# A weight stream of 591 slabs: TensorE waits for and releases each slab by halves, two token tiles in turn

## The chip, the cores and the metric

The kernel runs on one NeuronCore of a Trainium2 chip. The metric is the device time of one execution, in microseconds (us). Its engines are named as the profile names them: PE is TensorE (matmuls), with PEld for its weight loads; ACT is ScalarE; DVE is VectorE; POOL is GpSimd; SP is SyncE, which issues the loads of the weight stream.

## The reference

Two models of depth 2 run one after the other on one sequence of 256 tokens of width 1024, in float32. The first model's layer is a mixer (nine projections of 1024 columns, a gated recurrence over 8 heads, a short convolution, gates, an output projection) and a feed-forward part: dense in layer 0, and a mixture of 8 experts with the top 2 in layer 1. The second model's layer is feed-forward, mixer (gated MLP, pooling, sparse attention with a top-k, a convolution of 31 taps, four branches merged), feed-forward.

```python
def swiglu(h, w1, w3, w2):
    a = jnp.einsum('bsd,df->bsf', h, w1)
    b = jnp.einsum('bsd,df->bsf', h, w3)
    return jnp.einsum('bsf,fd->bsd', jax.nn.silu(a) * b, w2)

def moe_swiglu(h, router_w, w1, w3, w2):
    ...
    for e in range(N_EXPERTS):
        a = t @ w1[e]
        b = t @ w3[e]
        out = out + gates[:, e:e + 1] * ((jax.nn.silu(a) * b) @ w2[e])
    return out.reshape(bsz, seq, d)
```

What matters here is that all weights, some 620 MB, are read once, and that each is used in a matmul with few tokens.

## The kernel before

**The weight stream.** All large weights are laid out ahead of the launch as one array `W` of 591 slabs in the order of use. A slab is 128 partitions x 2048 float32 (`SLAB`), 1.05 MB, in two halves of 1024 columns (`HALF`), each loaded by a DMA of its own. A slab of an up or input projection holds four blocks of 512 columns (`CW`), one for each of four blocks of 128 of the contraction; the projection to 512 output columns takes two such slabs (`half` 0 and 1). A slab of a down projection holds two blocks of 128 rows with all 1024 output columns each, so that each half is one block of rows.

**Three engines handle each slab.** A float32 product is made of three matmuls in fp32r: the weight is split into a rounded high part and the rest, and the activations too, and high x high, high x low and low x high are added up in PSUM. For this SP loads a half into `raw` (`Sync.slabs`, L256 to L266), ACT copies it to `whi` in fp32r (`Scalar.hi`, L289 to L302), DVE subtracts `raw - whi` into `wlo` (`Vector.lo`, L727 to L738), and PE runs the three matmuls for each block and tile (`Tensor.slab`, L1299 to L1310). `raw`, `whi` and `wlo` have three slots each (`RING`), and ACT and DVE run two slabs ahead of PE (`LEAD`). The order in each engine's queue is written out by hand, so that an engine that waits for a slab holds up everything behind it.

**Who waits for whom.** There are four counters. A landing counts up `land{slot}{half}`. ACT's copy of a half waits for its landing and counts up `act_hi`. DVE's subtraction of a half waits for `act_hi` and counts up `dve_lo`. SP's load of a half waits for `dve_lo` of the same half three slabs earlier. So these three already work by halves. PE doesn't: it waits once for both halves of a slab (`dve_lo` at 2n + 2, L1304) and counts up `pe_slab` once, at the slab's last matmul (L1309); ACT waits for `pe_slab` of the slab three earlier before it copies either half (L297).

**How PE uses a slab.** `terms` is a list of (PSUM bank, high activations, low activations, columns of the slab, first, last). `columns` (L1312) makes it for up and input projections, `rows` (L1319) for down projections; two further lists stand in the mixer of the second model (its index projection and its branches). In all of them the token tile (128 tokens) is the outer loop and the block of the slab the inner one. Dense stages have two tiles, so 8 terms and 24 matmuls for a slab of an input projection; the experts gather their tokens into one tile, so 4 terms and 12 matmuls. Each tile accumulates in a bank of its own. An event that tells an evacuation that its banks are ready is always given with a slab's last matmul.

**The stages.** In order: the first mixer (48 slabs, `mixer1`), the dense feed-forward part (33), the mixer again (48), the experts (8 x 33 = 264 slabs), then for both layers of the second model feed-forward (33), mixer (33, `mixer2`), feed-forward (33). A feed-forward part is 22 slabs up and 11 down. In `up`, ACT does for every pair of slabs: two `hi`, the copy of the turned gate product of the pair before (L480), the SiLU of this pair (`gate`, L470 to L473), which waits for the pair's last matmul; DVE does two `lo`, the low part of the turned product (L943) and the product of the gate (L933 or L935). In the experts, PE also adds the previous expert's output into its tokens' places: `scatter` (L1551, L1552) with two matmul pairs for each tile, after the first pair of slabs for tile 0 and after the whole up projection for tile 1, and DVE adds the result to `X` (L993), in DVE's order behind the last `lo` and gate of the up projection. The down projection of the experts uses those banks, so PE waits for L993 before it starts. In the second model's mixer, DVE works through a top-k (L1162 to L1166) and through 31 taps of a convolution (L1179, L1182), with one `lo` after every six taps; PE needs the finished convolution at L1660.

The half of the stream that is ACT's, as it stands:

```python
            slot = self.slot()
            if self.n >= RING:
                act.wait_ge(k.of("pe_slab"), self.n - RING + 1)
            for h in range(2):
                part = slice(h * HALF, (h + 1) * HALF)
                act.wait_ge(k.of(f"land{slot}{h}"), 16 * (self.n // RING + 1))
                act.activation(k.whi[:, slot, part], k.raw[:, slot, part], ACT.Copy).then_inc(*k.up("act_hi"))
```

Of the kernel before, what the change touches and what calls it, by code (L numbers as in the profile page):

```python
# [38 lines left out]
HALF = SLAB // 2  # L39
RING = 3  # L40
# [245 lines left out]
class Scalar(Engine):  # L286

    def hi(self, count=1):  # L289

        act, k = self.eng, self.k
        for _ in range(count):
            if self.n == self.limit:
                return
            slot = self.slot()
            if self.n >= RING:
                act.wait_ge(k.of("pe_slab"), self.n - RING + 1)  # L297
            for h in range(2):
                part = slice(h * HALF, (h + 1) * HALF)
                act.wait_ge(k.of(f"land{slot}{h}"), 16 * (self.n // RING + 1))  # L300
                act.activation(k.whi[:, slot, part], k.raw[:, slot, part], ACT.Copy).then_inc(*k.up("act_hi"))  # L301
            self.n += 1  # L302
# [993 lines left out]
class Tensor(Engine):  # L1296

    def slab(self, terms, event=None):  # L1299

        pe, k = self.eng, self.k
        slot = self.slot()
        pe.wait_ge(k.of("dve_lo"), 2 * self.n + 2)  # L1304
        for ps, xh, xl, cols, first, last in terms:
            pe.matmul(ps, xh, k.whi[:, slot, cols], start=first, stop=False)  # L1306
            pe.matmul(ps, xh, k.wlo[:, slot, cols], start=False, stop=False)  # L1307
            mm = pe.matmul(ps, xl, k.whi[:, slot, cols], start=False, stop=last)  # L1308
        mm.then_inc(*k.up("pe_slab", event))  # L1309
        self.n += 1  # L1310

    def columns(self, half, bank, XH, XL, tiles=NT, step=1):  # L1312
# [735 lines left out]
```

## Time and profile before

| | |
|---|---|
| three runs | 3104.79, 3109.59, 3114.94 us; median 3109.59 |
| the profiled execution | 3106.7 us |
| its span, from the first to the last instruction | 3104.9 us |
| mean granted TensorE clock | 0.965 |
| busy: PE, PEld | 2898.1 us, 2376.6 us (13334 instructions each) |
| busy: DVE, ACT, POOL | 2062.2, 1696.0, 32.9 us |
| moved by DMA | 633.63 MB, mean 204 GB/s |
| the slabs' loads | 1182 of 512 KB, median 5.2 us from issue to landing |

All rows are of the one profiled execution. Its time is 1.8 us above its span, and 2.9 us below the median of the three runs. Matmuls are pipelined: a matmul's own length in the rows (0.39 us) is longer than the distance from its start to the next one's, and it is this distance, the pitch, that says how fast TensorE goes. The granted clock is a share of full speed: 1.00 is 2.4 GHz, 0.50 is 1.2 GHz.

### The profile page before, as it was taken

How to read it: one execution, taken by the hardware profiler on the slowest of the kernel's cores; microseconds unless marked ns; L12 is line 12 of the kernel's file. 1: busy time of each engine (PE TensorE's matmuls, PEld its weight loads, DVE VectorE, ACT ScalarE, POOL GpSimd, SP SyncE). 2: the span in 40 equal slices, each digit the busy share in tenths (PEclk: the TensorE clock that was granted, in tenths of full speed). 3: DMA queues.
4: the chain of work that ended last, by engine and by line, in shares of the span. 5: the costliest groups of instructions: out<-in, count | busy, mean ns of one | idle time of the engine just before them, and what ended most of it. 6: DMA issues, size and time to landing. Idle time of an engine off the chain costs nothing.

```text
span 3104.9 us, 34324 instructions
## 1 busy us (share of the span) xinstructions
PE 2898.1 (93%) x13334; PEld 2376.6 (77%) x13334; DVE 2062.2 (66%) x2910; ACT 1696.0 (55%) x2271; POOL 32.9 (1%) x55
## 2 busy tenths in 40 slices
PE   8998899999887999999999989989899999898998
PEld 6887688788765878777877768877778788776786
DVE  5566655656664898889888955468655455587553
ACT  5645354555523777677767754455454444555543
POOL 0000000000001000000000000000000000000000
PEclk9998899999987999999999989999999999999999
DMA  6443455454333999999989965544455555444453
GB/s 220 149 135 114 132 178 188 155 166 140 122 128 112 350 349 333 323 333 345 330 318 344 343 234 183 187 143 153 146 170 185 170 189 187 144 162 149 157 186 112
DMA packets 173658, 633.63 MB, mean 204 GB/s; under 512 B 19521, under 2 KB 19521, under 8 KB 173489
## 3 DMA queue, kind: packets, MB, share of 16 engines
q1 hardware_dynamic: 170752, 621.88, 59.0%
q0 software_dynamic: 2736, 9.49, 0.9%
q8 instruction: 107, 1.75, 0.2%
q14 instruction: 63, 0.51, 0.0%
HBM read 629.20 MB, written 2.10 MB: 203 GB/s over the span
## 4 chain that ended last, share of the span: by engine, by line
PE 78%; DVE 12%; DMA 4%; ACT 4%; issue 1%; SPq 0%; DVEq 0%; ACTq 0%; POOLq 0%
PE ps L1306 24%; PE ps L1308 23%; PE ps L1307 23%; DVE wlo L737 4%; DMA raw<-in_W 4%; PE ps L1418 2%; DVE CA L1182 2%; ACT whi L301 1%; PE ps L1495 1%; PE ps L1542 1%; PE ps L1338 1%; PE ps L1405 0%; PE ps L1404 0%; DVE XN L905 0%; DVE Z L1269 0%
## 5 line engine op out<-in xcount | busy, mean ns | idle before, releaser
L737 DVE TENSOR_TENSOR wlo<-raw,whi 128x1024 fp32r<-128x1024 f32 x1182 | 1394.0, 1221 | 560.4 <-ACT whi L301 550.8
L301 ACT ACTIVATE whi<-raw 128x1024 fp32r<-128x1024 f32 x1182 | 1197.8, 1057 | 600.8 <-PE ps L1308 547.7
L1306 PE MATMUL ps<-whi,XH 128*128 128x512 f32 (+1 forms) x2192 | 873.4, 398 | 41.2 <-DVE XL L755 17.3
L1307 PE MATMUL ps<-wlo,XH 128*128 128x512 f32 (+1 forms) x2192 | 859.0, 392 | 0.0
L1308 PE MATMUL ps<-whi,XL 128*128 128x512 f32 (+1 forms) x2192 | 859.0, 392 | 0.0
L1306 PEld LDWEIGHTS ps<-whi,XH 128*128 128x128 f32 x2192 | 418.8, 191 | 134.9 <-DVE XL L755 21.8
L1308 PEld LDWEIGHTS ps<-whi,XL 128*128 128x128 f32 x2192 | 417.6, 191 | 87.5
L1307 PEld LDWEIGHTS ps<-wlo,XH 128*128 128x128 f32 x2192 | 418.9, 191 | 82.8 <-issue 0.5
L1306 PE MATMUL ps<-whi,XEH 128*128 128x512 f32 x704 | 284.2, 404 | 1.4 <-DVE XEL L986 1.4
L1308 PE MATMUL ps<-whi,XEL 128*128 128x512 f32 x704 | 278.4, 395 | 0.0
L1307 PE MATMUL ps<-wlo,XEH 128*128 128x512 f32 x704 | 278.0, 395 | 0.0
L1306 PE MATMUL ps<-whi,GH 128*128 128x512 f32 x440 | 174.9, 397 | 0.0
L1308 PE MATMUL ps<-whi,GL 128*128 128x512 f32 x440 | 174.0, 395 | 0.0
L1307 PE MATMUL ps<-wlo,GH 128*128 128x512 f32 x440 | 174.0, 395 | 0.0
L1306 PE MATMUL ps<-whi,GH_ 128*128 128x512 f32 x352 | 147.8, 420 | 16.5 <-DVE X L993 16.5
L1308 PEld LDWEIGHTS ps<-whi,XEL 128*128 128x128 f32 x704 | 132.2, 188 | 31.6
L1306 PEld LDWEIGHTS ps<-whi,XEH 128*128 128x128 f32 x704 | 132.4, 188 | 30.0 <-DVE XEL L986 1.6
L1307 PEld LDWEIGHTS ps<-wlo,XEH 128*128 128x128 f32 x704 | 132.5, 188 | 28.7
L480 ACT ACTIVATE GH<-ps 128x512 fp32r<-128x512 f32 x55 | 32.9, 598 | 207.5 <-PE ps L1495 207.5
L943 DVE TENSOR_TENSOR GL<-ps,GH 128x512 fp32r<-128x512 f32 x55 | 38.0, 691 | 162.9 <-ACT GH L480 162.9
L1307 PE MATMUL ps<-wlo,GH_ 128*128 128x512 f32 x352 | 141.0, 400 | 0.0
L1308 PE MATMUL ps<-whi,GL_ 128*128 128x512 f32 x352 | 140.8, 400 | 0.0
(358 smaller groups left out, 2467.9 us busy)
## 6 DMA issues: line engine op xcount, KB each, us to landing
raw<-in_W SPq DMA_DIRECT2D x1182, 512.0 KB, 5.2
GP<-in_ffn_post_g POOLq DMA_DIRECT2D x4, 512.0 KB, 4.0
X<-in_x SPq DMA_DIRECT2D x1, 1024.0 KB, 5.0
skew<-RB POOLq DMA_DIRECT2D x4, 256.0 KB, 2.8
RB<-skew POOLq DMA_DIRECT2D x8, 128.0 KB, 2.5
GP<-in_mix_post_g POOLq DMA_DIRECT2D x2, 512.0 KB, 3.8
out<-X SPq DMA_DIRECT2D x1, 1024.0 KB, 4.0
mload<-in_cum_sums POOLq DMA_DIRECT2D x1, 768.0 KB, 8.5
```

The costliest lines, as they stand in the source:

```text
L301: act.activation(k.whi[:, slot, part], k.raw[:, slot, part], ACT.Copy).then_inc(*k.up("act_hi"))
L480: act.activation(GH[:, 2 * g:2 * g + 2, :], src, ACT.Copy).then_inc(*k.up("act_split", f"{T}.gh{g}"))
L737: dve.tensor_tensor(k.wlo[:, slot, part], k.raw[:, slot, part], k.whi[:, slot, part], ALU.subtract).then_inc(*k.up("dve_lo"))
L943: dve.tensor_tensor(GL[:, 2 * g:2 * g + 2, :], src, GH[:, 2 * g:2 * g + 2, :], ALU.subtract).then_inc(*k.up("dve_split", f"{T}.gl{g}"))
L1182: x = dve.scalar_tensor_tensor(out=CA[:, c, :], in0=HP[:, c, j:j + S], scalar=dw(c, j), in1=CA[:, c, :], op0=ALU.mult, op1=ALU.add)
L1306: pe.matmul(ps, xh, k.whi[:, slot, cols], start=first, stop=False)
L1307: pe.matmul(ps, xh, k.wlo[:, slot, cols], start=False, stop=False)
L1308: mm = pe.matmul(ps, xl, k.whi[:, slot, cols], start=False, stop=last)
L1338: mm = pe.transpose(bank[:, i * S + t * P:i * S + (t + 1) * P], src(2 * b + i, t), k.ident[:])
L1418: mm = pe.matmul(o, x, x, start=True, stop=True)
L1495: mm = pe.transpose(turned[:, fb, t * P:(t + 1) * P], GN[:, t, fb * P:(fb + 1) * P], k.ident[:])
L1542: mm = pe.matmul(k.ps[:, 6 + c // 4, (c % 4) * P:(c % 4 + 1) * P], k.XN[:, t, c * P:(c + 1) * P], k.PM[:, t, :], start=t == 0, stop=t == N ...
```

## The change

ACT waits for `pe_slab` ahead of each half in place of once for the slab, and the counter goes up by two for a slab. PE walks a slab's terms in two passes, one for each half of its columns. Ahead of each pass it waits for `dve_lo` of that half alone, and the last matmul of each pass counts up `pe_slab`; a stage's event stays with the second pass. With two tiles the order of the matmuls turns from tile 0 (all blocks), tile 1 (all blocks) to tile 0, tile 1 (the first half's blocks), tile 0, tile 1 (the second half's). With one tile it stays as it was. The matmuls themselves, their number and what they read and write are the same, and so are all loads, copies and subtractions.

```diff
@@ Scalar.hi
             slot = self.slot()
-            if self.n >= RING:
-                act.wait_ge(k.of("pe_slab"), self.n - RING + 1)
             for h in range(2):
                 part = slice(h * HALF, (h + 1) * HALF)
+                if self.n >= RING:
+                    act.wait_ge(k.of("pe_slab"), 2 * (self.n - RING) + h + 1)
                 act.wait_ge(k.of(f"land{slot}{h}"), 16 * (self.n // RING + 1))
                 act.activation(k.whi[:, slot, part], k.raw[:, slot, part], ACT.Copy).then_inc(*k.up("act_hi"))
@@ Tensor.slab
-        pe.wait_ge(k.of("dve_lo"), 2 * self.n + 2)
-        for ps, xh, xl, cols, first, last in terms:
-            pe.matmul(ps, xh, k.whi[:, slot, cols], start=first, stop=False)
-            pe.matmul(ps, xh, k.wlo[:, slot, cols], start=False, stop=False)
-            mm = pe.matmul(ps, xl, k.whi[:, slot, cols], start=False, stop=last)
-        mm.then_inc(*k.up("pe_slab", event))
+        for h in range(2):
+            pe.wait_ge(k.of("dve_lo"), 2 * self.n + h + 1)
+            for ps, xh, xl, cols, first, last in terms:
+                if cols.start // HALF != h:
+                    continue
+                pe.matmul(ps, xh, k.whi[:, slot, cols], start=first, stop=False)
+                pe.matmul(ps, xh, k.wlo[:, slot, cols], start=False, stop=False)
+                mm = pe.matmul(ps, xl, k.whi[:, slot, cols], start=False, stop=last)
+            mm.then_inc(*k.up("pe_slab", event if h else None))
         self.n += 1
```

## Rows read from the trace of the kernel before

**Rows 1.** The page, parts 1 and 4: busy time, and the chain that ended last

```profile
PE 2898.1 (93%) x13334; PEld 2376.6 (77%) x13334; DVE 2062.2 (66%) x2910; ACT 1696.0 (55%) x2271; POOL 32.9 (1%) x55
...
PE 78%; DVE 12%; DMA 4%; ACT 4%; issue 1%; SPq 0%; DVEq 0%; ACTq 0%; POOLq 0%
```

**Rows 2.** The page, part 5: busy us, mean ns | idle before, releaser

```profile
L737 DVE TENSOR_TENSOR wlo<-raw,whi 128x1024 fp32r<-128x1024 f32 x1182 | 1394.0, 1221 | 560.4 <-ACT whi L301 550.8
L301 ACT ACTIVATE whi<-raw 128x1024 fp32r<-128x1024 f32 x1182 | 1197.8, 1057 | 600.8 <-PE ps L1308 547.7
```

**Rows 3.** TensorE's waits: us in total, times, longest us

```profile
PE ps L1306 <- DVE X L993: 16.5, 7, 3.1
...
PE ps L1306 <- DVE wlo L737: 7.3, 4, 2.0
```

**Rows 4.** Windows: PE, PEld, DVE, ACT, POOL busy, then PEclk, DMA share, GB/s

```profile
400.00:480.00 80.00, 80.00 (x368) 66.28 (x367) 43.79 (x49) 36.74 (x50) 0.00 (x0) 1.00 0.59 193
1119.00:1149.00 30.00, 30.00 (x136) 24.20 (x135) 27.59 (x33) 24.48 (x32) 0.00 (x0) 1.00 0.99 369
1170.00:1190.00 20.00, 20.00 (x100) 16.64 (x99) 16.14 (x15) 13.08 (x14) 0.00 (x0) 1.00 0.89 298
```

**Rows 5.** Timeline of TensorE, dense up projection: start us, us

```profile
481.22 0.39 PE L1308 MATMUL ps<-whi,XL 128*128 128x512 f32 x1
481.44 0.39 PE L1306 MATMUL ps<-whi,XH 128*128 128x512 f32 x1
...
483.94 0.39 PE L1308 MATMUL ps<-whi,XL 128*128 128x512 f32 x1
484.16 0.39 PE L1306 MATMUL ps<-whi,XH 128*128 128x512 f32 x1
...
489.96 0.48 PE L1306 MATMUL ps<-whi,XH 128*128 128x512 f32 x1
490.28 0.39 PE L1307 MATMUL ps<-wlo,XH 128*128 128x512 f32 x1
```

**Rows 6.** Timeline of ScalarE, experts: two gates of an up projection, a down projection

```profile
1141.34 0.39 ACT L480 ACTIVATE GH_<-ps 128x256 fp32r<-128x256 f32 x1 [0.60 <-PE ps L1495]
...
1147.14 0.39 ACT L480 ACTIVATE GH_<-ps 128x256 fp32r<-128x256 f32 x1 [0.55 <-PE ps L1495]
...
1174.09 2.01 ACT L301 ACTIVATE whi<-raw 128x1024 fp32r<-128x1024 f32 x2 [1.24 <-PE ps L1308]
```

**Rows 7.** Timeline of ScalarE, VectorE, TensorE where an up projection ends

```profile
1252.58 2.20 ACT L301 ACTIVATE whi<-raw 128x1024 fp32r<-128x1024 f32 x2 [0.23 <-PE ps L1308]
...
1260.01 2.01 ACT L301 ACTIVATE whi<-raw 128x1024 fp32r<-128x1024 f32 x2 [1.86 <-DMA raw<-in_W]
...
1261.10 2.36 DVE L737 TENSOR_TENSOR wlo<-raw,whi 128x1024 fp32r<-128x1024 f32 x2 [1.50 <-ACT whi L301]
...
1264.05 1.22 DVE L993 TENSOR_TENSOR X<-ps,X 128x1024 f32<-128x1024 f32 x1
...
1261.90 0.40 PE L1552 MATMUL ps<-YL,PT 128*128 128x512 f32 x1
1265.36 0.47 PE L1306 MATMUL ps<-whi,GH_ 128*128 128x512 f32 x1 [3.06 <-DVE X L993]
```

**Rows 8.** Timeline of VectorE and TensorE, convolution of the second model's mixer

```profile
2117.39 2.36 DVE L737 TENSOR_TENSOR wlo<-raw,whi 128x1024 fp32r<-128x1024 f32 x2
2119.67 5.45 DVE L1182 SCALAR_TENSOR_TENSOR CA<-HP,pc,CA 128x256 f32<-128x256 f32 x12
...
2119.90 0.47 PE L1306 MATMUL ps<-whi,XH 128*128 128x512 f32 x1 [1.69 <-DVE wlo L737]
...
2136.14 1.13 PE L1660 MATMUL ps<-CA,ones 128*128 128x256 f32 x4 [2.79 <-DVE CA L1182]
```

**Rows 9.** Timeline of TensorE after an expert's stall, at half clock

```profile
1370.52 0.63 PE L1308 MATMUL ps<-whi,GL_ 128*128 128x512 f32 x1
1370.95 0.63 PE L1306 MATMUL ps<-whi,GH_ 128*128 128x512 f32 x1
```

## The prediction, made before the changed kernel ran

> **What bounds the kernel now.** The page comes first. TensorE is busy for 2898 of 3105 us, and most of the chain that ended last is its own matmuls; VectorE has 12% of that chain, DMA and ScalarE 4% each [rows 1]. So time can be won only in TensorE's 207 idle us (3105 - 2898), in stretches at half clock, or by cheaper matmuls. The stream that the change touches is the 1182 half slabs: a load of 512 KB (128 x 1024 numbers of 4 bytes), a ScalarE copy of 1.06 us and a VectorE subtraction of 1.22 us for each. ScalarE stood idle 548 us for TensorE before its copies, VectorE 551 us for ScalarE [rows 2]. Those two figures look like the prize, but idle time of an engine counts only if TensorE then waits for it. The view of TensorE's own waits says how often it does: 4 waits and 7.3 us for a subtraction of the stream, and 7 waits and 16.5 us for the add of L993, which stands behind the stream in VectorE's order [rows 3]. The rest of its idle time is for norms, transposes and splits that no slab feeds.
>
> Next the windows by stage. In a dense stage (two token tiles) DMA is busy 0.59 of the time and TensorE all of it; in the experts (one tile, half the matmuls for the same bytes) DMA is busy 0.99 at 369 GB/s in the up projection and 0.89 in the down projection [rows 4]. A slab is 1.05 MB. In the up projection the copies L480 ahead of two gates start 5.80 us apart, at 1141.34 and 1147.14 [rows 6], which is two slabs: 2.1 MB in 5.8 us ask for 361 GB/s, nearly what DMA gives. So the experts are the only place where the stream is nearly as slow as TensorE.
>
> **The change, part by part.** (1) **Marks.** 591 slabs get one more wait and one more signal in TensorE's stream. A wait that has been met and a signal already stand at each slab's end: the matmul at 483.94 signals, the one at 484.16 has waited, and the pitch is 0.22 us, as it is inside a slab (481.22 to 481.44) [rows 5]. I take 0. The clock of the rows reads to 0.01 us, so the bound is 0.01 x 591 = 5.9 us slower, and there is no reason for a gain. The Trainium skill speaks against the change here ("TensorE: Matmul & The Clock Gate", The cost: per-tile semaphore tail): there each further signal on a matmul adds some 26 ns, which would be 591 x 0.026 = 15 us; the rows above show no such step at the signals that are there already, though those come at the end of a slab too.
>
> (2) **Order of the matmuls.** The same 24 matmuls of a dense slab run as tile 0, tile 1, tile 0, tile 1 in place of tile 0, tile 1, so there are two more changes of bank in 327 slabs. The change of tile is just the pair 481.22 to 481.44, 12 matmuls before the slab's end [rows 5], with no step in it. I take 0; bound 654 x 0.01 = 6.5 us slower. In the experts the order stays. Banks are signalled ready only by a slab's last matmul, before and after, so no evacuation comes earlier.
>
> (3) **Earlier release, dense stages.** The copy of a slab's first half may start half a slab (2.7 us) earlier, the second half's as before; ScalarE then has 1.06 us less left after the slab's end, VectorE finishes about 1.1 us earlier, and SyncE's next load, which waits for that subtraction, goes out as much earlier. DMA has room for it at 0.59 [rows 4], and GpSimd's few loads are far off. What is queued behind on ScalarE (gates, evacuations) waits for the end of a later slab anyhow. TensorE doesn't wait for slabs there, as two lie ready ahead. Worth 0; the cover is that lead of a slab or more, some 5 us against about 3.5 us of copy and subtraction. A loss is excluded, since nothing is asked to be ready sooner than before.
>
> (4) **Mixer of the second block, twice.** Here VectorE is the bound: a slab's two subtractions (2.36) and twelve taps of the convolution (5.45) make 7.8 us against 5.45 us of matmuls. TensorE waits for two slabs, 1.69 us for the first (four such waits in both mixers make up the 7.3 us) [rows 3], and then 2.79 us for the last tap [rows 8]. With half waits it starts each of the two slabs one subtraction (1.14 us) earlier. But the next work needs VectorE's last tap, whose time doesn't move, as those subtractions don't wait for ScalarE. So 4 x 1.14 = 4.6 us are won and all given back in a longer idle of about 3.9 us before L1660. I take 0. A longer idle may bring a stretch at half clock: bound 1.5 us slower for each mixer (priced below).
>
> (5) **Experts.** In the down projection ScalarE waits 1.24 us for a slab's end before a pair of copies [rows 6]; that goes, and the stream gets about 1.2 us ahead, where nobody is waiting. What counts is the end of the up projection: TensorE's last scatter starts at 1261.90, the add L993 runs only at 1264.05, behind two late subtractions, and TensorE resumes at 1265.36, after 3.06 us idle [rows 7]. Back from there: the subtractions at 1261.10 waited for a copy, and that for a load (1.86 us), not for TensorE. Over the whole up projection ScalarE's first copy of a pair follows its gate, which waits for a whole slab; only the second one waits for TensorE, and for 0.23 us [rows 7]. The lead won in the down projection is lost again at these gates, since three slots can't hold more. I take 0.2 us for each of 7 stalls: 1.4 us faster. The far bound: if VectorE were never late, the idle would be the add behind the last scatter, about 1.22 plus 0.1 us, so 16.5 - 7 x 1.3 = 7.4 us to win, and the half clock that follows three of the seven stalls. At half clock the pitch is 0.43 instead of 0.23 us [rows 9]; over the 3.3 us that such a stretch lasts that is 3.3 x (1 - 0.23/0.43) = 1.5 us, three times 4.5. Together 12 us faster; the near bound is 0.
>
> **Sum.** The profiled execution took 3106.7 us (span 3104.9 and 1.8 around it): 3106.7 - 1.4 = 3105.3. The median of the three runs is 2.9 us above it, so 3108.2, say **3108**. A difference under 0.3% (9.3 us) can't be told from no change here: the runs shown spread over 10 us.
>
> **Rivals.** *A: the experts' stalls go.* If the DMA engines are kept busy from the down projection on, the lead isn't lost and the late loads land before they are asked for. For it: 0.89 in the down projection, so there is room, and loads that are late at its end [rows 4, 7]. Against: loads wait for slots, slots for gates. It gives the 12 us of (5): 3109.6 - 12 = 3098, and it is the only way that I see to a clear gain. Chance 0.17.
>
> *B: the half clock comes to more stalls.* The change moves idle time about: shorter before slabs, longer before L1660. Of the seven expert stalls four were followed by full clock, and so were some four of like length in the two mixers. Were all eight to fall, 8 x 1.5 = 12 us slower: 3120. It decides once six of them fall and none of the others is spared. For it: stalls of like length come with and without half clock, so it turns on little. Against: chance works both ways, and the experts' stalls don't grow. Chance 0.06.
>
> *C: a mark in the middle of a slab costs.* If the array ran empty at the signal or the weight load couldn't go ahead past the wait, each would cost up to what the dearest spot between matmuls of a slab shows: after the transposes the pitch is 0.32 (489.96 to 490.28) instead of 0.23 [rows 5], 0.09 x 591 = 53 us, 3161. The pitch of 0.22 over a signal and a met wait in the same rows speaks against it. By the skill's 26 ns above it would be some 3123. Chance 0.03.
>
> *D: nothing reaches TensorE at all*, (5) included: 3109.6, within my forecast. The forecast with D has 0.74.
>
> **How the numbers follow.** Faster by over 0.3% is A: 0.17. Slower is B and C: 0.09. Same 0.74. The range takes in most of A below and part of B and the bounds of (1) and (2) above: 3097 to 3117.
>
> **What would show it.** Right: ScalarE's idle time for TensorE before L301 falls from 548 us by roughly 200 to 300, and that doesn't reach the span; TensorE's wait for wlo falls from 7.3 to about 3 us and its wait for CA L1182 grows by as much; the seven waits for L993 stay at 15 to 17 us; the pitch over the new mark is 0.22 to 0.23; DMA in the up projection stays at 0.99. Wrong: the waits for L993 fall near 9 us (A), windows of the experts with a lower granted clock (B), a step at the twelfth matmul (C), or more busy time of TensorE for the same 13334 matmuls.

## The result and the profile after

The changed kernel took 3118.19 us (median of 8 runs, 3113.66 to 3124.32), the kernel before 3111.07 us (8 runs, 3101.48 to 3119.64). The ratio is 1.0027, with the interval 1.0014 to 1.004. The means of the eight runs lie 8.4 us apart, so the change loses about 8 us. That is less than the 0.3% (9.3 us) under which the prediction said that nothing could be told from no change; with eight runs of each kernel the interval reaches some 4 us to either side, and it doesn't hold 1. The time is 1 us above the range of 3097 to 3117. The same kernel timed once more (below) gave 1.0024.

The page of the changed kernel: its head, the busy times and the chain that ended last.

```profile
span 3115.6 us, 34912 instructions
...
PE 2904.3 (93%) x13334; PEld 2381.7 (76%) x13334; DVE 2067.9 (66%) x2910; ACT 1707.3 (55%) x2271; POOL 32.9 (1%) x55
...
PE 75%; DVE 15%; DMA 5%; ACT 4%; issue 1%; SPq 0%; ACTq 0%; DVEq 0%; POOLq 0%
```

Against [rows 1] two things stand out. TensorE has the same 13334 matmuls but is busy 6.2 us longer (2904.3 against 2898.1), and in the chain 3% have gone from TensorE to VectorE. The second isn't the loss: a kernel below without the loss has TensorE at 75% too. The granted clock says where most of the 6.2 us come from: 235 us of the span are at half clock, 222 before, and there the pitch is 0.43 us in place of 0.23 [rows 9]. By stage, TensorE is busy 2.3 us longer in the experts (6.9 us more at half clock) and 4.0 us longer behind them (13.3 us more). TensorE's idle time grew by the rest, from 207 to 211 us. The two add up to the 10.7 us by which the span grew.

The same page, the two groups of the slabs' preparation (busy us, mean ns | idle before, releaser).

```profile
L737 DVE TENSOR_TENSOR wlo<-raw,whi 128x1024 fp32r<-128x1024 f32 x1182 | 1401.1, 1223 | 475.0 <-ACT whi L301 465.2
L301 ACT ACTIVATE whi<-raw 128x1024 fp32r<-128x1024 f32 x1182 | 1210.7, 1061 | 509.5 <-PE ps L1311 396.7
```

ScalarE's idle time for TensorE fell from 547.7 to 396.7 us and VectorE's for ScalarE from 550.8 to 465.2 [rows 2], and nothing of it reached the span. What reached it stands in TensorE's own waits (us in total, times, longest):

```profile
PE ps L1309 <- DVE X L993: 20.2, 7, 5.0
...
PE ps L1663 <- DVE CA L1182: 7.9, 2, 4.0
...
PE ps L1309 <- DVE wlo L737: 6.2, 4, 2.0
```

The seven waits for L993, at the end of each expert's up projection, are 20.2 us in place of 16.5 [rows 3]. The worst, 5.03 us, in the timeline of ScalarE, VectorE and TensorE after the change (start us, us; in brackets the idle time before):

```profile
1572.56 1.06 ACT L301 ACTIVATE whi<-raw 128x1024 fp32r<-128x1024 f32 x1 [0.86 <-DMA raw<-in_W]
...
1573.65 2.52 DVE L737 TENSOR_TENSOR wlo<-raw,whi 128x1024 fp32r<-128x1024 f32 x2 [0.70 <-ACT whi L301]
1573.85 1.06 ACT L301 ACTIVATE whi<-raw 128x1024 fp32r<-128x1024 f32 x1 [0.23 <-DMA raw<-in_W]
...
1576.74 1.22 DVE L993 TENSOR_TENSOR X<-ps,X 128x1024 f32<-128x1024 f32 x1
...
1578.06 0.77 PE L1309 MATMUL ps<-whi,GH_ 128*128 128x512 f32 x1 [5.03 <-DVE X L993]
```

It is the stall of [rows 7], only longer: a load lands late, ScalarE copies behind it, VectorE subtracts behind that, and the add of L993 that TensorE needs stands last. Both of the last two copies waited for their loads. The 0.77 us of the first matmul behind it, in place of 0.47 in [rows 7], is the half clock.

What is new shows in the chain that ended last, ahead of that stall (start us, us, what), here of the changed kernel:

```profile
1566.76 7.01 DMA raw<-in_W
1573.77 0.02 issue
1573.79 0.02 ACTq L300
1573.80 0.04 issue
1573.85 1.07 ACT whi L301
```

A second half's copy in the kernel before:

```profile
1145.37 6.47 DMA raw<-in_W
1151.84 0.02 issue
1151.86 1.07 ACT whi L301
```

Before, this copy starts 0.02 us after its load has landed. Now an instruction of ScalarE's queue (`ACTq L300`, the wait for the landing) stands between, and the copy starts 0.08 us after. The reason is in the instruction counts.
```profile
span 3104.9 us, 34324 instructions
```

which is one for each slab from the fourth on (591 - 3): the wait for `pe_slab` that the second half now has. And of the two waits, the one written last (the landing) is the separate instruction, L300, while the copy itself carries the wait for `pe_slab`, long met where the load is late. In the kernel before only the first halves had two waits, and its chain shows the separate one there:

```profile
1773.87 5.95 DMA raw<-in_W
1779.82 0.02 issue
1779.84 0.02 ACTq L300
1779.85 0.04 issue
1779.90 1.07 ACT whi L301
```

Over all copies that a load held, the trace of before has a mean of 0.088 us from landing to copy for first halves and 0.023 for second ones, that of after 0.082 and 0.081.

Whether these 0.06 us matter depends on how often a load holds a copy. ScalarE's waits before L301 (us in total, times, longest), kernel before:

```profile
ACT whi L301 <- PE ps L1308: 547.7, 247, 7.2
...
ACT whi L301 <- DMA raw<-in_W: 48.3, 90, 1.9
```

and changed kernel:

```profile
ACT whi L301 <- PE ps L1311: 396.7, 274, 4.2
...
ACT whi L301 <- DMA raw<-in_W: 111.8, 202, 2.7
```

The waits for loads went from 90 to 202. Copies asked for earlier meet loads that can't come earlier; that isn't all of it, as the kernel below that only adds the second wait has 166 and 143 in its two profiles. The window 1511 to 1577, the up projection of the experts with the longest stall (busy us of PE, PEld, DVE, ACT, POOL with counts, then PEclk, DMA share, GB/s), before:

```profile
1511.00:1577.00 66.00, 63.92 (x286) 51.22 (x284) 61.65 (x68) 52.44 (x67) 0.00 (x0) 1.00 0.97 352
```

and after:

```profile
1511.00:1577.00 66.00, 62.01 (x275) 49.01 (x273) 58.18 (x66) 49.70 (x64) 0.00 (x0) 0.99 0.95 338
```

DMA is less busy and moves 338 in place of 352 GB/s. Loads that are issued later would look like this: SyncE's next load into a slot waits for the subtraction, that for the copy, and that for the landing. The experts as a whole, from the start of their first matmul with XEH to the start of their last with GH_, took 823.8 us before and 829.5 after. What lies behind the experts grew by 5.4 us in these two executions, from 1286.7 to 1292.1.

### The profile page after: what moved, and what is told of

Its sections match the earlier page's. It is cut to its first block, busy times and chain, and to the rows that moved or that the text cites. A ratio compares the mean times of both kernels' runs of the same rounds, so it can differ in the third digit from the quotient of the medians.

```text
span 3115.6 us, 34912 instructions
## 1 busy us (share of the span) xinstructions
PE 2904.3 (93%) x13334; PEld 2381.7 (76%) x13334; DVE 2067.9 (66%) x2910; ACT 1707.3 (55%) x2271; POOL 32.9 (1%) x55
## 4 chain that ended last, share of the span: by engine, by line
PE 75%; DVE 15%; DMA 5%; ACT 4%; issue 1%; SPq 0%; ACTq 0%; DVEq 0%; POOLq 0%
PE ps L1309 22%; PE ps L1311 22%; PE ps L1310 22%; DVE wlo L737 6%; DMA raw<-in_W 5%; PE ps L1421 2%; DVE CA L1182 2%; ACT whi L301 1%; PE ps L1498 1%; PE ps L1545 1%; PE ps L1341 1%; PE ps L1408 0%; PE ps L1407 0%; DVE XN L905 0%; DVE Z L1269 0%
## 5 line engine op out<-in xcount | busy, mean ns | idle before, releaser
L737 DVE TENSOR_TENSOR wlo<-raw,whi 128x1024 fp32r<-128x1024 f32 x1182 | 1401.1, 1223 | 475.0 <-ACT whi L301 465.2
L301 ACT ACTIVATE whi<-raw 128x1024 fp32r<-128x1024 f32 x1182 | 1210.7, 1061 | 509.5 <-PE ps L1311 396.7
L1309 PE MATMUL ps<-whi,XH 128*128 128x512 f32 (+1 forms) x2192 | 872.7, 398 | 40.5 <-DVE XL L755 17.8
L1309 PEld LDWEIGHTS ps<-whi,XH 128*128 128x128 f32 x2192 | 418.8, 191 | 133.9 <-DVE XL L755 21.9
L1309 PE MATMUL ps<-whi,XEH 128*128 128x512 f32 x704 | 284.4, 404 | 1.4 <-DVE XEL L986 1.4
L1309 PE MATMUL ps<-whi,GH 128*128 128x512 f32 x440 | 174.9, 397 | 0.0
L1309 PE MATMUL ps<-whi,GH_ 128*128 128x512 f32 x352 | 148.6, 422 | 20.2 <-DVE X L993 20.2
L1309 PEld LDWEIGHTS ps<-whi,XEH 128*128 128x128 f32 x704 | 132.4, 188 | 30.9 <-DVE XEL L986 1.6
```

The source lines that it names most:

```text
L737: dve.tensor_tensor(k.wlo[:, slot, part], k.raw[:, slot, part], k.whi[:, slot, part], ALU.subtract).then_inc(*k.up("dve_lo"))
```

## The experiments

All kernels compute the whole of the reference. Each was timed in five rounds against the kernel before on the same chip; beside the median stands the ratio with its interval. "Experts" is that stretch in the one profiled execution of a kernel; it scatters by several us between executions (all its values stand in a table at the end of this section), so the ratios decide. The kernel before measured 3108.1 to 3111.3 us (medians) in these series.

### The parts, one at a time

*ScalarE's second wait alone.* The kernel before, with its own met wait for `pe_slab` asked again ahead of the second half:

```
-            if self.n >= RING:
-                act.wait_ge(k.of("pe_slab"), self.n - RING + 1)
             for h in range(2):
...
+                if self.n >= RING:
+                    act.wait_ge(k.of("pe_slab"), self.n - RING + 1)
                 act.wait_ge(k.of(f"land{slot}{h}"), ...)
```

> TensorE as before. Only ScalarE waits a second time, ahead of a slab's second half, for the count it has already seen. Theory 1 (the added wait of ScalarE costs): in the changed kernel's profile a copy of a second half that waits for its load starts 0.08 us after the landing, before it was 0.02; here it must be 0.08 too, the up projections of the experts move about 340 GB/s in place of 351, the seven waits for L993 come to about 20 us in place of 16.5, and the time is 4 to 7 us above before (ratio 1.0013 to 1.0023). Theory 2 (the half clock and the mixer's longer stall cost, ScalarE's wait nothing): ratio 1.000, waits for L993 16 to 17 us.

Measured: 3110.23 us, ratio 1.0004 (0.9995 to 1.0013). Landing to copy is 0.08 us for both halves, the waits for L993 are 19.3 us and the experts 832.8, as in the changed kernel, but the time doesn't follow: theory 1 had asked for 1.0013 or more. Once more:

> The kernel before with ScalarE's second, met wait, once more. Theory 1: experts 828 to 834 us, ratio 1.001 to 1.002. If the first timing (1.0004) holds and the experts come out at 825 here, the second wait costs only together with the earlier copies of the change.

3111.53 us, 1.0005 (0.9994 to 1.0016), and this time the waits for L993 are 16.8 us and the experts 826.0, with the same 0.08 us from landing to copy. The wait by itself measures 1 to 2 us, and the intervals reach from nothing to 5 us.

*TensorE's half waits and the order of tiles, one mark a slab.* As the change, with `mm.then_inc(...)` once, behind the loop over `h`, and ScalarE as before.

> TensorE waits by halves and takes two tiles in turn, but signals once a slab, and ScalarE waits once. Theory 1: the waits for L993 as before, 16 to 17 us, DMA in the up projections 351 GB/s; the wait of L1663 or its like for the last tap grows from 2.8 to 3.95 us in both mixers, and the whole is 0 to 3 us slower. Theory 2: this carries nearly all of the loss, 6 to 9 us (ratio 1.002 to 1.003), with more stretches at half clock than before (24, 221.7 us in total).

3113.58 us, 1.001 (0.9999 to 1.0021): 3 us, with an interval from 0 to 6.5 us. Theory 2, which put 6 to 9 us here, is out at all but its lower end.

*The marks without use.* TensorE waits for whole slabs (`2 * self.n + 2`), tiles in turn, a mark after each half; ScalarE waits once a slab, for `2 * (self.n - RING) + 2`.

> TensorE takes two tiles in turn and signals each half, but waits for whole slabs, and ScalarE waits once, for the second mark. So ScalarE's and VectorE's work comes when it did before. If a mark in the middle of a slab costs TensorE nothing (forecast): pitch across the mark 0.22 to 0.23 us, experts 822 to 826, ratio within 0.9995 and 1.0005. If each costs some 0.02 us (rival C at the skill's figure): TensorE's busy time 10 us or more up and the ratio above 1.003.

3110.95 us, 1.0007 (0.9995 to 1.0019). 591 more signals and the new order measure 2 us, 6 at most.

*The marks used.* The changed kernel, but TensorE waits for whole slabs.

> The changed kernel, but TensorE waits for whole slabs. ScalarE has its two waits, and copies a first half once half the slab is used. Theory 1: experts 828 to 833 us and the waits for L993 19 to 21 us, as in the changed kernel; the waits for the last tap (L1182) back at 2.8 us; ratio 1.001 to 1.0025. If the half waits of TensorE are what costs: ratio 1.000 to 1.0005.

3111.22 us, 1.0009 (0.9998 to 1.002).

*By place.* The whole change for the experts' 264 slabs alone, then for all the others alone (a helper counts the marks; it decides on `MOE_BASE <= n < MOE_BASE + NE * FF_SLABS`).

> The whole change, but for the 264 slabs of the experts alone. Theory 1: 4 to 7 us slower, waits for L993 near 20 us. Theory 2: within 1 us of before, since neither the order of the matmuls nor the convolution's stall is touched.

> The whole change, but for the 327 slabs outside the experts alone. Theory 1: 1 to 4 us slower (the mixers' part); waits for L993 16 to 17 us. Theory 2: 6 to 9 us slower. If both parts cost, this and the kernel with the experts alone add up to the 7 to 8 us of the whole.

Experts alone: 3113.51 us, 1.0013 (1.0003 to 1.0023). The rest alone: 3109.3 us, 1.0004 (0.9995 to 1.0014). So a loss shows where the stream is nearly as slow as TensorE, and none is seen in the dense stages and the second model's mixers. But the two together make 1.0017, less than the whole change's 1.0027 and 1.0024. The intervals leave room for an equal sum; whether the parts cost more together than one by one isn't settled by these runs.

*TensorE's half waits in the second model's mixers alone* (66 slabs, one mark a slab):

> The kernel before, but TensorE waits by halves, and takes two tiles in turn, in the two mixers of the second model (66 slabs), with one mark a slab. If the longer idle ahead of the last tap and the half clock behind it are the second cost: waits for CA L1182 grow from 2.8 to 3.95 us (or come earlier with a half clock stretch between), the part behind the experts takes 1288 to 1290 us in place of about 1286, ratio 1.0003 to 1.001. If they aren't: 1286 and 1.000.

3110.33 us, 1.0006 (0.9994 to 1.0018). TensorE's waits for the stream and for the last tap (L1665 is L1660 of the kernel before):

```profile
PE ps L1311 <- DVE wlo L737: 5.1, 4, 2.0
PE ps L1665 <- DVE CA L1182: 4.7, 2, 2.4
```

The wait for the last tap didn't grow to 3.95 us but came out at 2.3 and 2.4, with a stretch at half clock 9 us ahead of it, the case that the expectation had in brackets. The part behind the experts took 1285.6 us, so it lost nothing.

### The order of two waits

*The change with the landing asked first.* This is the experiment that decides. Two source lines change places, nothing else:

```
             for h in range(2):
                 part = slice(h * HALF, (h + 1) * HALF)
+                act.wait_ge(k.of(f"land{slot}{h}"), 16 * (self.n // RING + 1))
                 if self.n >= RING:
                     act.wait_ge(k.of("pe_slab"), 2 * (self.n - RING) + h + 1)
-                act.wait_ge(k.of(f"land{slot}{h}"), 16 * (self.n // RING + 1))
```

The instructions are as many (34912). Only, now the wait for `pe_slab` is the separate one and the copy itself waits for the landing.

> The changed kernel with ScalarE's two waits ahead of each copy in the other order: landing first, then TensorE's mark. In the traces so far a copy held up by its load starts 0.08 us after the landing where it has two waits and 0.02 where it has one. Theory 1 (the second wait stands between landing and copy as an instruction of its own): with the landing waited for by the copy itself the 0.08 falls to about 0.02 for both halves, the experts take 822 to 826 us as in kernels whose ScalarE wasn't touched (824, 826, 822) and not 830 to 833, and the whole is at 1.000 to 1.0015 of before. Theory 2 (marks and order in the experts cost by themselves): experts at about 830 and the ratio at 1.0027 as in the changed kernel.

3107.14 us, 0.9993 (0.998 to 1.0006): the loss is gone. Its chain (start us, us, what):

```profile
1143.75 6.71 DMA raw<-in_W
1150.46 0.02 issue
1150.48 1.07 ACT whi L301
```

ScalarE's waits in it,

```profile
ACT whi L301 <- PE ps L1311: 400.2, 275, 4.3
ACT whi L301 <- DMA raw<-in_W: 92.8, 194, 2.0
```

TensorE's wait for L993 in it,

```profile
PE ps L1309 <- DVE X L993: 15.9, 7, 3.1
```

and the window of before:

```profile
1511.00:1577.00 66.00, 63.10 (x282) 50.65 (x281) 60.99 (x68) 51.84 (x66) 0.00 (x0) 1.00 0.96 348
```

The copy follows its load by 0.02 us again. ScalarE still waits 194 times for a load, as with the change, yet TensorE's waits for L993 are 15.9 us, the rate is 348 GB/s, and the experts take 822.8 us. So it is not that copies are asked for earlier that costs, but in which order the two waits stand. What the order changes in the trace is only where the 0.06 us go: copies held by TensorE's mark now start 0.085 us after it, in place of 0.022 with the change as it was, and those held by a load start 0.023 us after it, in place of 0.08. The same delay costs nothing behind TensorE's mark.

Both kernels again, on another chip and beside each other:

> The changed kernel itself, once more, so that it and the next one are timed in the same rounds. If the loss is real: ratio 1.0015 to 1.0035, landing to copy 0.08 us, experts 828 to 832 us. If the first measurement was partly luck: below 1.001.

> The changed kernel with the landing waited for by the copy itself, once more beside it. Theory 1: 0.999 to 1.001, at least 4 us below the changed kernel in the same rounds; experts 822 to 827 us. Theory 2: the same as the changed kernel.

The change 3117.64 us, 1.0024 (1.0012 to 1.0036); landing first 3110.87 us, 1.001 (0.9995 to 1.0024). The waits for L993 are 21.0 and 16.8 us, the experts 832.0 and 823.5. The two intervals overlap in part; the pair below doesn't.

*Landing first, by place.* The changed kernel with the landing first for the experts' slabs only, then for all the others only.

```
+                if experts:
+                    act.wait_ge(k.of(f"land{slot}{h}"), ...)
                 if self.n >= RING:
                     act.wait_ge(k.of("pe_slab"), 2 * (self.n - RING) + h + 1)
+                if not experts:
+                    act.wait_ge(k.of(f"land{slot}{h}"), ...)
```

> The changed kernel, with the copy itself waiting for the landing for the experts' slabs alone. If the loss by the order of the waits sits in the experts: experts 822 to 829 us, ratio 1.0000 to 1.0010, as with the order turned everywhere (0.9993 and 1.0010). If it sits in the dense stages: 1.002 or more.

> The changed kernel, with the order turned for the 327 slabs outside the experts alone. If the loss sits in the experts: experts 829 to 834 us, ratio 1.0015 to 1.0027, as in the changed kernel. If it sits outside: 1.0010 or less.

Experts only: 3110.2 us, 0.9992 (0.998 to 1.0003). The others only: 3117.58 us, 1.0025 (1.0013 to 1.0038), the loss in full. TensorE's wait in the first,

```profile
PE ps L1313 <- DVE X L997: 16.7, 7, 4.4
```

and in the second (four lines of source were added, so L1313 is L1309 of the changed kernel and L997 its L993):

```profile
PE ps L1313 <- DVE X L997: 19.8, 7, 4.3
```

The chain of the second, in the experts:

```profile
1767.03 6.05 DMA raw<-in_W
1773.09 0.02 issue
1773.11 0.02 ACTq L304
1773.12 0.04 issue
1773.17 1.07 ACT whi L305
```

A warning on single executions: the second's profiled one took 3109.16 us, 8 us under its own median, and its span (3107.3 us) is shorter than the first's (3109.1). Whoever compares only those two profiles gets the sign wrong; the eleven runs of each don't leave it open: the two intervals don't touch.

*Landing first on partial changes.* The experts-only change, and the kernel with the marks used but whole waits on TensorE, each with the two lines swapped:

> The change for the experts alone, with the copy itself waiting for the landing. Theory 1: experts 822 to 826 us, ratio 0.999 to 1.0005 (the same with the waits in the change's order was 1.0013). Theory 2 (marks or half waits cost the experts something): experts 829 or more, ratio 1.001 or more.

> TensorE marks each half and takes two tiles in turn, but waits for whole slabs; ScalarE's copy waits for the landing itself. It has neither of the two costs. Experts 822 to 826 us, the second model's part about 1286 us, waits for the last tap 2.8 us; ratio 0.9985 to 1.0000. Faster than before by more than 0.1% only if the earlier copies shorten the waits for L993 below 15 us.

3108.73 us, 0.9991 (0.9978 to 1.0005), beside 1.0013 with the landing last; and 3110.83 us, 1.0000 (0.9988 to 1.0011), beside 1.0009. The second pair of intervals overlaps widely. The experts took 828.4 and 828.1 us, not the 822 to 826 that theory 1 had asked for.

*The kernel before with the landing first.* It has two waits at first halves only:

```
-            if self.n >= RING:
-                act.wait_ge(k.of("pe_slab"), self.n - RING + 1)
             for h in range(2):
...
                 act.wait_ge(k.of(f"land{slot}{h}"), ...)
+                if h == 0 and self.n >= RING:
+                    act.wait_ge(k.of("pe_slab"), self.n - RING + 1)
```

> The kernel before with only the order of ScalarE's two waits ahead of a first half turned round. Theory 1: landing to copy of a first half falls from 0.09 to 0.02 us, the experts to 815 to 822 us, ratio 0.998 to 0.9995. Theory 2: no difference.

3108.35 us, 0.9998 (0.9985 to 1.0011). First halves now start 0.025 us after the landing in place of 0.089, and it wins nothing. The experts took 829.0 us, where 815 to 822 were expected. So where only first halves are delayed, taking the 0.06 us away brings nothing that can be measured.

### More waits in the kernel before

Met waits for `act_hi` and `dve_lo` beside the one for `pe_slab`, ahead of both halves (36088 instructions: one more for each copy than the change has); then those and met waits for the five other landing semaphores too (`act.wait_ge(k.of(f"land{j}{g}"), 16)`; 38440 instructions, two more for each copy):

> The kernel before, with ScalarE waiting for three met counts beside the landing ahead of each half (TensorE's mark, and two that were reached long ago), where it had one or none. A larger dose. Theory 1: landing to copy grows to about 0.2 us on both halves, the experts to 845 us or more, and the whole is over 10 us slower (ratio above 1.003). Theory 2: ratio 1.000 to 1.001, since these waits are all met and ScalarE is idle 45% of the time.

> The kernel before with eight met waits of ScalarE beside the landing and TensorE's mark, ahead of each half. One more made landing to copy 0.08 us, three made it 0.11; this should make it about 0.2. Theory 1 (a later copy lengthens the loop load, copy, subtraction, load, and the experts' up projections have no slack for it): experts 838 us or more, ratio 1.004 or more. If 0.2 us is still hidden: experts 822 to 828, ratio within 1.001, and then the 0.06 us of the change can't be the cause either.

3112.59 us, 1.0012 (0.9999 to 1.0025), landing to copy 0.11 us; and 3114.41 us, 1.0014 (1.0002 to 1.0025), with 0.12 us for first halves and 0.10 for second ones. Both had been expected over 1.003. The second kernel missed its aim: I had meant to double the delay, but the copy starts hardly later. In its trace most copies held by a load have four separate waits ahead of them, and only the last of the four ends after the landing; the others had run while ScalarE was idle. A delay of the size of the change's or a little more, in an otherwise old kernel, measures from 1 to 5 us.

*The experts in all kernels.* Each value is of one profiled execution; beside it stand TensorE's waits for L993 in total.

| kernel | ratio | experts, us | waits for L993, us |
|---|---|---|---|
| before | | 823.8 | 16.5 |
| the change; again | 1.0027; 1.0024 | 829.5; 832.0 | 20.2; 21.0 |
| landing first outside the experts only | 1.0025 | 829.3 | 19.8 |
| landing first; again | 0.9993; 1.001 | 822.7; 823.5 | 15.9; 16.8 |
| landing first in the experts only | 0.9992 | 824.7 | 16.7 |
| ScalarE's second wait alone; again | 1.0004; 1.0005 | 832.8; 826.0 | 19.3; 16.8 |
| half waits, one mark a slab | 1.001 | 826.1 | 17.8 |
| marks unused | 1.0007 | 827.7 | 16.6 |
| marks used | 1.0009 | 835.0 | 19.5 |
| marks used, landing first | 1.0000 | 828.1 | 17.8 |
| change in the experts only | 1.0013 | 830.1 | 19.1 |
| the same, landing first | 0.9991 | 828.4 | 18.5 |
| change outside the experts only | 1.0004 | 822.1 | 15.4 |
| half waits in the mixers only | 1.0006 | 829.3 | 18.4 |
| before, landing first | 0.9998 | 829.0 | 18.1 |
| more waits; still more | 1.0012; 1.0014 | 826.8; 838.0 | 17.7; 21.4 |

Three of these kernels run the experts with the code of before: 823.8, 822.1 and 829.3 us. So a difference of 6 us in one execution each places nothing, and of the readings above only those hold in which the ratios agree. In the six executions of the whole change the experts do separate by the order of the waits there, 829 to 832 against 823 to 825 us.

## Why the prediction was wrong where it was

**The step that failed is (5), the experts.** It forecast 0.2 us won at each of 7 stalls, 1.4 us in all, with a far bound of 12 us faster and a near bound of 0. So a loss was not among its ends, as (3) had excluded one "since nothing is asked to be ready sooner than before". Measured is a loss of about 8 us, and what decides on it is the order of ScalarE's two waits in the experts: the loss is there with the landing last in the experts alone, and gone with the landing first in the experts alone. The reason given in (3) was true, and beside the point. Nothing is asked for sooner, but the change also adds an instruction: the wait on ScalarE ahead of the second half. I costed the waits and signals on TensorE, which measured next to nothing, and left this one out of the sum, though it delays each second half held by a load from 0.02 to 0.08 us after its landing. The profile of before could have told me: the chain shows the separate wait at first halves and none at second halves, and the window with DMA at 0.99 [rows 4] suggests that in the experts load, copy and subtraction form a loop with little slack. How 0.06 us at such a place add up to 8 us stays open, as said next.

**What is shown and what isn't.** Shown: with the landing asked last in the experts the whole change loses 7 to 8 us in three series (1.0027, 1.0024, 1.0025), and with the landing asked first there none of three differs from the kernel before by more than its interval (0.9993, 1.001, 0.9992), with the same waits, marks, matmuls and number of instructions. The means of the runs differ from those of before by 8.4, 8.2 and 7.3 us, and by -1.6, 2.9 and -1.9. That the 0.06 us between landing and copy are what the order acts by is argued: it is the only difference that the traces show, but the cost doesn't grow with it (0.10 to 0.12 us in the kernels with more waits, and 4 to 5 us). Not settled is why the same 0.06 us cost less in an otherwise old kernel (1.0004 and 1.0005). In the changed kernel a load holds 86 first and 116 second halves, in its second profile 70 and 99, in the kernel with ScalarE's second wait alone 71 and 95, before 42 and 48. The product 116 x 0.06 = 7.0 us looks like the answer, but 99 held second halves go with a loss of 8.2 us and 95 with one of about 1, so the sum by counts doesn't hold. That the half marks and half waits make the loop tighter is a guess.

**(1) Marks: right.** The timeline of TensorE over the new mark, which stands at the matmul of 484.41, the slab's twelfth:

```profile
484.41 0.39 PE L1311 MATMUL ps<-whi,XL 128*128 128x512 f32 x1
484.63 0.39 PE L1309 MATMUL ps<-whi,XH 128*128 128x512 f32 x1
```

The pitch is 0.22 us, as inside a slab [rows 5]. Over the whole trace of the changed kernel, wherever the pitch between two of the stream's matmuls is under 0.30 us (which leaves out half clock and stalls), its mean is 0.230 us over a signal and 0.229 elsewhere. The kernel with marks that nobody uses differs by 1.0007 (0.9995 to 1.0019), at most 6 us. Rival C is out, the 53 us by the dearest pitch as well as the 15 us. The 15 us came from the 26 ns for each signal that the Trainium skill gives ("TensorE: Matmul & The Clock Gate", The cost: per-tile semaphore tail) for small matmuls packed side by side into the array, a case other than this one; the trace shows no such cost for a signal between whole matmuls that follow each other.

**(2) Order of the tiles: right**, in the same kernel. **(3) Dense stages: right in the number.** The change there alone gives 1.0004 (0.9995 to 1.0014).

**(4) The second model's mixers: the mechanism was right, the half clock was the part left open.** The timeline of TensorE after the change, last bracket the wait:

```profile
2125.20 0.47 PE L1309 MATMUL ps<-whi,XH 128*128 128x512 f32 x1 [1.92 <-DVE wlo L737]
...
2132.88 0.50 PE L1309 MATMUL ps<-whi,XH 128*128 128x512 f32 x1 [1.99 <-DVE wlo L737]
...
2142.58 1.65 PE L1663 MATMUL ps<-CA,ones 128*128 128x256 f32 x3 [3.96 <-DVE CA L1182]
```

The idle time before L1663 is 3.96 us; about 3.9 was forecast, and 2.79 stood before [rows 8]. Half clock followed it this time: three matmuls in 1.65 us, where four took 1.13 [rows 8]. The waits for `wlo` fell less than forecast, from 7.3 to 6.2 us in place of about 3. One part of that was a slip of mine: the second slab's start moves 1.14 us earlier, but the end of the slab before it does too, so its wait stays what it was (1.99 us now; before, the row is

```profile
2127.57 0.50 PE L1306 MATMUL ps<-whi,XH 128*128 128x512 f32 x1 [1.95 <-DVE wlo L737]
```

in the kernel before). Only the first wait of each mixer can shrink, and 7.3 - 2 x 1.14 = 5.0 us would be left. The kernel with half waits in the mixers alone has just that, 5.1 us. The other part is the clock: in the changed kernel the first wait is 1.92 us and not 0.55, because TensorE ran dry earlier. A window 50 us ahead of it, before and after (busy us of PE, PEld, DVE, ACT, POOL with counts, then PEclk, DMA share, GB/s):

```profile
2070.00:2080.00 10.00, 7.58 (x29) 6.21 (x30) 9.76 (x25) 3.36 (x5) 1.82 (x2) 0.83 0.45 141
```

```profile
2070.00:2080.00 10.00, 7.14 (x34) 5.70 (x33) 9.79 (x17) 5.57 (x7) 2.70 (x2) 1.00 0.49 162
```

Before, 3.4 us of it were at half clock; after, none. In the nine kernels with half waits in the mixers this holds for all 18: the first wait is 0.54 or 0.55 us in the 12 that have this stretch at half clock, and 1.91 to 1.93 us in the 6 that don't. And in all 18 the distance from the end of that first wait to L1663 or its like is 17.4 us, where it was 16.2 before (2136.14 - 2119.90 [rows 8]): TensorE starts one subtraction earlier and is held to VectorE's last tap all the same, as forecast. The wait for the last tap is 3.9 to 4.0 us, or 2.3 to 2.4 where half clock came 9 us ahead of it and stretched the matmuls. In time it comes to little: what lies behind the experts took 1286.7 us before and 1292.1 after, but the kernels with half waits in the mixers show anything from 1285.6 to 1292.1, and the one with nothing else measured 1.0006 (0.9994 to 1.0018).

**The signs to look for.** ScalarE's idle time for TensorE fell by 151 us, less than the 200 to 300 forecast, since part of it became waiting for loads (63.5 us more). DMA stayed where it was in the window of [rows 4], 1119 to 1149 (1.00 after, 0.99 before), but not where the longest stall is (from 0.97 to 0.95 in the window above), and the waits for L993 left their 15 to 17 us. "More busy time of TensorE for the same 13334 matmuls" stood in the list of what would make the forecast wrong, and it came, 6.2 us. But it doesn't go with the loss alone: the kernel with the marks used was busy for 2904.3 us too, at a ratio of 1.0009.

**The rivals.** A (the stalls go, 3098) didn't happen even with the landing first: L993 stayed at 15.9 and 16.8 us, not near 9. B (more half clock, 3120) came nearest in the number, and half clock did grow by 13 us of the span, with 6.2 us more busy time. But most of that growth lies behind the experts, where the kernel with the landing first had as much of it and lost nothing. And the expert stalls, which were said not to grow, did. So B named a part of what happened and not its cause, and that its number is near is luck.

## What to carry to other kernels

A wait that is always met can still matter: here a copy takes one wait by itself, and the second becomes an instruction of its own that may stand between the event that comes last and the work. Where two waits are needed, look in the chain for which of them stands alone, and try the order in which the work itself waits for the one that comes last. It won 7 us in the changed kernel and nothing in the kernel before, so it is to be measured each time. And when a change adds a wait on an engine, cost it there too, above all in a stage where the DMA engines are nearly full.

## What the runs showed of the hardware that was not expected

The order of two wait lines in the source decides whether a copy starts 0.02 or 0.08 us after a landing, and in the changed kernel that is worth 7 us, in 3110 us: 3117.64 against 3110.87 for the order everywhere, and 3117.58 against 3110.2 for the experts' order alone, each pair on one chip. Whichever of TensorE's mark and the landing is asked first, its held copies start after 0.02 us, and those held by the other after 0.08. Further met waits ahead of the landing add little (0.10 to 0.12 us in all, with one and with three more instructions for each copy than the change has), since all but the last of them end before the landing. No version here beats the kernel before: the best ratios are 0.9991, 0.9992 and 0.9993, and all their intervals hold 1.
